# Attention units of a two-layer decoder trunk: score products moved ahead of the cross-attention memory's products

## The reference

```python
for layer in range(DEPTH):
    z = rms_norm(h, norm_mix[layer]) @ w_in[layer]
    ...
    y = jnp.concatenate([_rms(y_ssm), _rms(y_conv), _rms(y_nsa)], axis=-1) * mix_out_norm[layer]
    h = h + y @ w_out[layer]
    h = h + cross_attention(rms_norm(h, norm_cross[layer]), rms_norm(mem, norm_mem[layer]), ...)
    hn = rms_norm(h, norm_ffn[layer])
    if layer % 2 == 0:
        h = h + swiglu(hn, ffn_w_up[layer // 2], ffn_w_down[layer // 2])
    else:
        h = h + moe_swiglu(...)          # top 2 of 8 experts

# in nsa_mixer, for each query head, with a causal bias by distance
s_s = jnp.einsum('bkgqd,bkqsd->bkgqs', qc, k_g) * scale + bias_s
p_s = masked_softmax(s_s, mask_s[:, :, None])
o_s = jnp.einsum('bkgqs,bkqsd->bkgqd', p_s, v_g)
# in cross_attention
k, v = jnp.split(memn @ w_kv, 2, axis=-1)      # memory tokens x 512 columns
```

## Time and profile before

| | us |
|---|---|
| median of 3 runs | 1283.74 (1282.45 to 1287.72) |
| the profiled execution: its own time | 1285.27 |
| the profiled execution: its span | 1283.4 |
| TensorE busy in the span | 1239.3 (97%) |
| VectorE / ScalarE / GpSimd busy | 700.8 / 429.7 / 99.6 |

### The profile page before, as it was taken

The page is one execution under the profiler, slowest core; times in us unless marked ns, Lnnn a source line. Parts: engine busy times, 40 slices in busy tenths (PEclk is TensorE's granted clock), DMA queues, the critical chain, the costliest instruction groups (busy, mean ns, idle before and its releaser), DMA issues.

```text
span 1283.4 us, 49041 instructions
## 1 busy us (share of the span) xinstructions
PE 1239.3 (97%) x21626; PEld 1053.9 (82%) x21626; DVE 700.8 (55%) x1629; ACT 429.7 (33%) x884; POOL 99.6 (8%) x157
## 2 busy tenths in 40 slices
PE   7999998999999999999899999999999999999888
PEld 5755566887887776556699999999999999999887
DVE  6885435647966366642455555545555555554445
ACT  4526413001002132642333333333333334333232
POOL 1270010000000045011000000000000000000010
PEclk9999999999999999999999999999999999999999
DMA  9521025243532543205989999999999999999994
GB/s 370 234 81 54 1 99 212 99 159 138 197 148 115 200 175 123 88 1 203 371 360 429 423 426 426 425 426 425 427 426 426 424 427 424 426 427 424 426 424 163
DMA packets 36283, 360.97 MB, mean 281 GB/s; under 512 B 4131, under 2 KB 5795, under 8 KB 11260
## 3 DMA queue, kind: packets, MB, share of 16 engines
q1 hardware_dynamic: 33488, 354.86, 67.0%
q10 hardware_dynamic: 2156, 3.19, 0.7%
q0 software_dynamic: 576, 2.10, 0.4%
HBM read 356.77 MB, written 3.36 MB: 281 GB/s over the span
## 4 chain that ended last, share of the span: by engine, by line
PE 81%; DMA 9%; DVE 6%; issue 2%; ACT 1%; SPq 1%; POOL 0%; ACTq 0%; DVEq 0%
PE bank L2470 25%; PE bank L1837 19%; PE bank L2487 12%; DMA ring<-moe_w_dram 7%; PE bank L2413 6%; PE bank L2190 4%; PE bank L1845 2%; PE bank L2457 2%; PE bank L2119 1%; PE bank L1996 1%; SPq L544 1%; PE bank L2208 1%; PE bank L2178 1%; DMA ring<-ffn_w_dram 1%; PE bank L1882 1%
## 5 line engine op out<-in xcount | busy, mean ns | idle before, releaser
L2470 PE MATMUL bank<-R,ring 128*64 128x80 f32 x11264 | 426.4, 233 | 11.2 <-DVE ring L1731 9.7
L2470 PEld LDWEIGHTS bank<-R,ring 128*64 128x64 f32 x11264 | 404.8, 137 | 17.8 <-DVE ring L1731 15.3
L1837 PE MATMUL bank<-ring 128*128 128x128 f32 (+2 forms) x1776 | 287.7, 321 | 1.5 <-ACT ring L635 0.9
L1837 PEld LDWEIGHTS bank<-ring 128*128 128x128 f32 x1776 | 242.8, 191 | 49.3 <-issue 36.6
L2487 PE MATMUL bank<-zz,ring 128*64 128x80 f32 x5632 | 225.8, 233 | 0.0
L942 ACT ACTIVATE ring<-ring 128x1024 f32<-128x1024 f32 x160 | 169.0, 1057 | 134.8 <-PE bank L2487 134.8
L2487 PEld LDWEIGHTS bank<-zz,ring 128*64 128x64 f32 x5632 | 208.9, 138 | 0.0
L1782 DVE SCALAR_TENSOR_TENSOR zz<-zz,bank 128x80 f32<-128x80 f32 x176 | 42.0, 238 | 173.9 <-PE bank L2470 173.1
L1731 DVE COPY ring<-ring 128x1024 f32<-128x1024 f32 x160 | 110.0, 688 | 19.6 <-DMA ring<-moe_w_dram 19.6
L947 ACT ACTIVATE sqx<-bank 128x80 f32<-128x80 f32 x176 | 41.8, 238 | 223.9 <-PE bank L2470 223.2
L1735 DVE COPY ring<-ring 128x1024 f32<-128x1024 f32 x160 | 109.8, 686 | 0.2 <-DVE R L1721 0.2
(11 more groups left out here) (340 smaller groups left out, 1152.8 us busy)
## 6 DMA issues: line engine op xcount, KB each, us to landing
ring<-moe_w_dram SPq DMA_DIRECT2D x160, 1536.0 KB, 21.4
ring<-ffn_w_dram SPq DMA_DIRECT2D x11, 3072.0 KB, 10.2
ring<-w_in_dram SPq DMA_DIRECT2D x6, 2048.0 KB, 7.9
extra<-moe_w_dram SPq DMA_DIRECT2D x8, 1536.0 KB, 23.2
ring<-w_out_dram SPq DMA_DIRECT2D x4, 2048.0 KB, 7.8
ring<-w_small_dram SPq DMA_DIRECT2D x2, 3072.0 KB, 10.6
ring<-w_x_dram SPq DMA_DIRECT2D x2, 3072.0 KB, 10.8
ring<-w_in_dram SPq DMA_DIRECT2D x2, 2144.0 KB, 15.3
```

Of the source, the lines that this page charges most:

```text
L1837: i = pe.matmul(out_ap, a, b, start=(k == 0), stop=(k == n - 1))
L2470: e = pe.matmul(pb[out_bank][c0:c0 + 64, 0:CAP], half[:, P * k + c0:P * k + c0 + 64], xg[:, k], start=(k == 0), stop=(k == KT - 1), tile_p ...
```

## The change

In each odd unit the call of `scores` for the next pair now stands ahead of the call of `mem_part`. Nothing else is touched. Only the units in `MEM_AT` (3, 5, 7, 9 and 11) have both calls, so five places per layer change.

```diff
@@ -2232,10 +2232,10 @@
                         banks.open(pe, f"pT0{v + 1}_{l}")
                         for _ in range(FILLERS):
                             pe.matmul(ps(f"pT0{v + 1}_{l}")[:, 0:256], ident, cst[:, 0:256], start=True, stop=True)
+                    if v % 2 and v + 3 < 2 * NH:
+                        scores((v + 3) // 2)
                     if v in MEM_AT:
                         mem_part(f"mkv0_{l}", 0, 0, 512, MEM_AT[v])
-                    if v % 2 and v + 3 < 2 * NH:
-                        scores((v + 3) // 2)
                 values(2 * NH - 1)
```

## The result

The changed kernel takes 1305.75 us (median of 4 runs, 1304.23 to 1315.37) against 1284.57 us (4 runs) of the kernel before: a ratio of 1.018, 95% interval 1.016 to 1.020. I forecast slower, 1298 with a range of 1290 to 1303; it is slower by half as much again as I said, and outside the range. The profiled execution took 1305.89 us, its span is 1304.0 us, 20.6 more than before, and its mean granted clock is 0.984 after 0.994.

What follows compares the result with a forecast made beforehand. The prediction took TensorE, with 81% of the chain that ended last, to bound the kernel. Order 11.5 us plus clock 3.0 gave 14.5 us on 1285.27, 1299.8; as a median 1298, slower by 1.1%, range 1290 to 1303.

Steps and rivals of the forecast that it cites:

- the cover of the scores' wait: Memory's products ahead of the scores cover most of TensorE's wait for VectorE's L1486; the change puts them behind it.
- All five terms: Delays at units 3, 5, 7, 9 and 11: +0.44, +1.05, +1.91, +2.35 and 0 us, 5.75 a layer.
- unit 14's wait: TensorE's 1.79 us wait ahead of unit 14's transposes, forecast to stay as it is.
- The two rivals that needed absorption or cover by the transposes: One layer's 5.75 us absorbed, 1291 us, chance 0.12; memory's products cover a wait of the transposes, 1284 to 1288, chance 0.09.
- the faster one: Rival: earlier scores let VectorE and ScalarE get ahead, unit 14's wait and low clock go; 1277 us, chance 0.03.
- the sum: Order's cost over the five places, unit by unit: 5.75 us a layer, 11.5 us for both layers.
- unit 9's idle of 1.8 us: Sign: TensorE idle between unit 9's two score products, about 1.8 us.
- 7 to 9: Sign: total of L2119's waits for L1486 in layer 0, 2.9 us before, should become about 7 to 9 us.
- I take one a layer, +3.0 us together: Clock term: one extra fall to half clock in each layer, 1.5 us apiece; zero to three a layer held possible.
- 5.7 to 8 and 11 to 16: Sign: output projection starts later by 5.7 to 8 us in layer 0 and 11 to 16 in layer 1.
- unit 5's smaller gap: New TensorE idle of 1.20 us ahead of unit 5's first score, smaller than the gaps of units 7 and 9.
- the clock falls at every new gap: Rival: three clock falls a layer at 1.5 us each, 1304 us, chance 0.10.

Runs made afterwards that it cites:

- the kernel with the dummy products: Changed kernel plus dummy products ahead of the scores in units 5 (two), 7 (four) and 9 (three): 1297.19 us, 1.009 of the kernel before.
- unit 9's kernel: Kernel before, with scores ahead of the memory's three slices in unit 9 alone: ratio 1.0056 (1.0036 to 1.0076).
- unit 7 alone: Kernel before, with scores ahead of the memory's two slices in unit 7 alone: ratio 1.0052 (1.0035 to 1.0069).
- the first of the better tables: Kernel before, memory still ahead of scores, slices redealt: one in unit 5, three in 7, three in 9, one in 13: 1279.87 us, ratio 0.996.

## Why the prediction was wrong

**Right: the place and the mechanism.** The memory's slices were the cover of the scores' wait. All five terms came out in the trace at full clock (the kernel with the dummy products): +0.34, +0.96, +1.82, +2.37 and -0.10 us against +0.44, +1.05, +1.91, +2.35 and 0. VectorE kept its distance to TensorE's L2100, unit 14's wait kept its size, and nothing behind absorbed the delay. The two rivals that needed absorption or cover by the transposes are out, and so is the faster one. Two sizes beside the sum were too large: unit 9's idle of 1.8 us was 1.15, because the first product alone takes 1.05 us and I had let it take half of that, and TensorE's weight loads of L2119 waited 6.2 us for L1486 (98 to 160 us), not 7 to 9. The sum hangs on neither, since it starts from the second product.

**Wrong: the size of the clock term.** "I take one a layer, +3.0 us together" is the step that failed. It put two more stretches of 3.4 us on the kernel, 6.8 us more at the low level. The two layers' units had 3.4 us at the low level twice before, and six low windows of 29.4 us after, three of them twice as long as the one that I had seen. Of the 20.6 us of span the order is 10.8 (twice 5.4, measured with the gaps filled), and 9.8 are left. From 6.8 to about 30 us at the low level is 23 us more, and at the 0.41 us that unit 9's kernel shows, 9.5. The two agree; at the slopes of 0.28 to 0.35 that whole executions show it would be 6.5 to 8 us, most of the rest. My price of 1.5 us for 3.4 at the low level, 0.44 for each, was near; how long the clock is low was not. This is also why the output projections started 11.2 and 19.1 us later and not 5.7 to 8 and 11 to 16.

Two assumptions made it small. I gave unit 5's smaller gap no fall of its own; it was 1.13 us in the trace and a low stretch of some 6.8 us began at its end (window 115.70), and with it moved alone the clock fell behind it in both layers. And I priced each gap as the one fall seen behind unit 14, singly. The places moved one by one sum to 17.8 us, all together cost 23.0. The intervals are wide enough that nearly all of the difference may be chance, but it has the sign of gaps that help each other: units 5, 7 and 9 follow within 25 us, and unit 7's gap brought a fall in one layer of two when it was moved alone and in all four layers of the two profiled executions with all five moved. Unit 9's went the other way, one of two and none of four. That gaps help each other is not shown. The rival "the clock falls at every new gap", at 1304 with a chance of 0.10, comes nearest in number and partly by luck: the clock fell at two of the three new gaps in each layer, not at unit 9's, and three of the four falls lasted twice as long as the rival had them.

The rule cited from the page "TensorE: Matmul & The Clock Gate" of the Trainium skill (section "A second HAM failure mode: psum-queue depth-cycling") was the better guide. By that rule small gaps in a row can make the clock swing; the trace agrees, with the level going 1.00, 0.50, 1.00, 0.50 from unit 5 to unit 8, and filling the gaps ended it.

**Open:** what decides whether a gap brings a fall, and why one execution falls more often than another. The same program had spans of 1302.3 us at 0.984 and 1313.5 us at 0.975.

## What to carry to other kernels

Work that waits for nothing belongs ahead of an instruction whose operand or bank comes late, on an engine that runs in order; before dealing such work out, measure each hidden wait from the start of a row to the start of the next, and put as much cover there as the wait is long. A new gap on TensorE must be priced twice, for its own length and for the clock behind it, and here the second price (9.8 us of span) was nearly as large as the first (10.8). To tell the two apart, fill the gap with dummy products: if the kernel gets faster by doing more, it was the clock.

## What the runs showed of the hardware

The clock fell behind gaps far shorter than the stretches that followed them: 1.13 us idle in unit 5, then 6.8 us at half the clock (3.4 in layer 1, behind 1.20 us), and 1.72 us idle in unit 7, then 6.8. Such a gap brings a fall often and not always: unit 14's 1.80 us was followed by none in layer 0 of three profiled kernels (the dummies, unit 7 alone, unit 9 alone). What tells the cases apart was not tried. A us at the low level cost 0.41 us in the attention units and 0.28 to 0.35 over whole executions, less than the half that a wholly busy TensorE would lose. Half-array products cost as much alone as in pairs (1.05 and 1.06 us). And in some executions, of several kernels, the clock stayed low for most of 13.5 us where the experts start:

```profile
624.60:638.10 13.50, 12.69 (x99) 10.87 (x99) 5.29 (x22) 1.79 (x4) 0.00 (x0) 0.51 0.88 345
```

That is from the first of the better tables; the kernel before had a mean clock of 1.00 from 600 to 640 us in its profile. By an estimate with 0.22 us for each us (the 1.5 for 6.8 behind the units of layer 1) to 0.41, such a stretch is worth some 3 to 5.5 us, as much as many of the differences measured here, which is why a single execution can't rank these kernels.
